# Gate product of the second layer as seven block products (Strassen), with its first two units between the last transposes of the rows, in a two-layer encoder kernel

## What is computed

```python
for i in range(2):
    h = rmsnorm(x, g_pre[i])
    o = mixer_i(h)                      # attention, convolution or Fourier branches, output projection
    x = x + rmsnorm(o, g_post[i])       # called x1 below
    x = x + sigmoid(x @ w_ple_gate[i]) * (p[i] @ w_ple[i])
```

## Time and profile before

| | |
|---|---|
| median of 3 runs | 2020.82 us |
| profiled execution, its own time | 2011.86 us |
| its span, first to last instruction | 2010.1 us |
| PE busy | 1934.5 us, 96% |
| PE weight load, DVE, ACT, POOL busy | 80%, 54%, 32%, 37% |
| mean granted TensorE clock | 0.990 |
| last product of the output projection ends, gate's last embedding ends | 1829.7, 2006.1 us |

### The profile page before, as it was taken

The page is one execution under the profiler, slowest core; times in us unless marked ns, Lnnn a source line. Parts: engine busy times, 40 slices in busy tenths (PEclk is TensorE's granted clock), DMA queues, the critical chain, the costliest instruction groups (busy, mean ns, idle before and its releaser), DMA issues. The chain is left out here.

```text
span 2010.1 us, 26242 instructions
## 1 busy us (share of the span) xinstructions
PE 1934.5 (96%) x9856; PEld 1615.1 (80%) x9856; DVE 1094.2 (54%) x1639; ACT 652.4 (32%) x1339; POOL 745.0 (37%) x540
## 2 busy tenths in 40 slices
PE   4999999999989999999989999999999999999999
PEld 3788888887889788788777888777989897887887
DVE  5599999736768217415753100366777773265211
ACT  6111212211668332212222111123777774322000
POOL 0111121132687444545533132223635362544521
PEclk9999999999989999999999999999999999999999
DMA  4102333443566546534311222484221224565322
GB/s 170 64 11 68 137 93 108 143 143 112 181 236 229 199 160 229 183 107 145 116 52 40 72 85 89 155 308 140 59 54 48 62 78 145 176 240 185 114 94 80
DMA packets 144176, 256.73 MB, mean 128 GB/s; under 512 B 30593, under 2 KB 69249, under 8 KB 144066
## 3 DMA queue, kind: packets, MB, share of 16 engines
q1 hardware_dynamic: 144066, 255.25, 38.6%
HBM read 166.93 MB, written 88.28 MB: 127 GB/s over the span
## 5 line engine op out<-in xcount | busy, mean ns | idle before, releaser
L589 DVE SCALAR_TENSOR_TENSOR ie_acc<-ie_u,ie_wconv,ie_acc 128x1551 f32<-128x1551 f32 x120 | 249.7, 2081 | 3.2
L187 POOL TENSOR_TENSOR w_lo_part<-w_raw,w_hi_part 128x1024 fp32r<-128x1024 f32 x24 | 67.8, 2827 | 331.1 <-ACT w_hi_part L179 331.1
L169 POOL TENSOR_TENSOR w_hi_part<-w_raw,zero 128x1024 fp32r<-128x1024 f32 x56 | 108.0, 1928 | 174.6 <-DMA w_raw<-wall 167.6
L1425 PE MATMUL op_ps<-w_hi_part,rows_hi 128*128 128x512 f32 x384 | 157.1, 409 | 5.1 <-DVE rows_lo L1153 2.6
L1632 DVE SCALAR_TENSOR_TENSOR gt_x<-gt_tanh,gt_ps_p 128x512 f32<-128x512 f32 x48 | 33.0, 688 | 230.1 <-PE gt_ps_p L1665 211.2
L324 PE MATMUL ie_ps<-rows_hi,w_hi_part 128*128 128x512 f32 x384 | 150.4, 392 | 3.9 <-DVE w_lo_part L553 3.8
L1652 PE MATMUL gt_ps<-w_hi_part,rows_hi 128*128 128x512 f32 x384 | 153.3, 399 | 0.0
L1425 PE MATMUL op_ps<-w_hi_part,rows_lo 128*128 128x512 f32 x384 | 152.4, 397 | 0.0
L324 PE MATMUL ie_ps<-rows_hi,w_lo_part 128*128 128x512 f32 x384 | 152.3, 397 | 0.0
L1425 PE MATMUL op_ps<-w_lo_part,rows_hi 128*128 128x512 f32 x384 | 152.0, 396 | 0.0
L1652 PE MATMUL gt_ps<-w_lo_part,rows_hi 128*128 128x512 f32 x384 | 152.0, 396 | 0.0
(11 more groups left out here) (254 smaller groups left out, 4926.8 us busy)
## 6 DMA issues: line engine op xcount, KB each, us to landing
w_raw<-wall SPq DMA_DIRECT2D x84, 512.0 KB, 4.8
op_in<-x SPq DMA_DIRECT2D x24, 512.0 KB, 4.4
x<-op_in SPq DMA_DIRECT2D x24, 512.0 KB, 3.0
gt_x<-x SPq DMA_DIRECT2D x48, 256.0 KB, 3.3
pro_x<-x SPq DMA_DIRECT2D x12, 512.0 KB, 8.8
op_in<-attn SPq DMA_DIRECT2D x24, 256.0 KB, 3.0
o_half<-op_ost SPq DMA_DIRECT2D x24, 256.0 KB, 2.2
gt_p_raw<-p_fm SPq DMA_DIRECT2D x48, 128.0 KB, 3.2
```

What stands on the lines that cost most here:

```text
L169: pool.tensor_tensor(hi, raw, g.zero[:, 0:1].broadcast_to([P, QCOLS]), ALU.add).then_inc(g.w_hi, 1)
L187: pool.tensor_tensor(g.W[1][:, pair % 2, off:off + QCOLS], g.raw[:, n % 2, :], g.W[0][:, pair % 2, off:off + QCOLS].bitcast(F32), ALU.subt ...
L589: dve.scalar_tensor_tensor(acc[:], ubuf[:, cc, s:s + CW], wconv[:, cc, s:s + 1], acc[:], ALU.mult, ALU.add).then_inc(taps, 1)
L1425: mm = pe.matmul(product_at(c * NT + t), g.XT[a][:, k, t * P:(t + 1) * P], w_at(g, name, m, k * HALF, HALF), start=k + a + m == 0, stop=k ...
```

## The change

The second layer's gate product is computed by Strassen's method in Winograd's form. x1 is cut in four blocks (first 768 rows against last 768, first 512 of the inner dimension against last 512), and so is W (rows against columns, B11 to B22). Seven products of 768x512 by 512x512 take the place of eight, in passes named after their left operand: A11, A12, S2, S3, S1, S4, A22. A pass has 6 units (a tile of 128 rows by 512 columns), so there are 42 units of 12 matrix instructions (4 pieces by 3) in place of 24 of 24. The passes A12, S1, S4 and A22 complete a result each time; the embedding (6 instructions), tanh and the two DVE instructions follow there, 24 times as before.

What else it adds or moves:
- In `out_proj` ACT copies the turned x1 whole (`copy_rows`) in place of `split_hi`, DVE's `split_lo` is gone, and both split the left operand of the first seven units there, one per step from step 6 on. Afterwards each engine's loop over n splits the left operand of unit n+7 (`high` on ACT, `low` on DVE) into a ring of 8.
- DVE also makes the sums S1 to S4 of x1's blocks (24 instructions of 128x512, both inputs in SBUF), and adds the units up: 42 instructions of 128x512 with one input in PSUM (`consume`).
- The right operands T2, T3, T1 and T4 are sums of W's blocks. SP loads blocks of 1 MB and 512 KB for them, POOL sums (10 instructions of 128x1024), ACT takes the high part (10, `w_high`), POOL the low part (10). The second half of the gate weights is no longer split as before.
- PE turns the last two tiles of x1 after units 0 and 1 of the gate.
- SP's list has the block loads between the stores of finished units.

The core of the diff:

```diff
+SEVEN = ("A11", "A12", "S2", "S3", "S1", "S4", "A22")
+PAIRS_OF_TILES = NT // 2
+NU = len(SEVEN) * PAIRS_OF_TILES
+RING, AHEAD = 8, 7
...
+    def source(self, n):
+        i, j = divmod(n, PAIRS_OF_TILES)
+        name = SEVEN[i]
+        return {"A11": self.row(0, 0, j), "A12": self.row(0, 1, j), "S2": self.s2(j), "S3": self.row(0, 0, j),
+                "S1": self.row(1, 0, j), "S4": self.row(0, 1, j), "A22": self.row(1, 1, j)}[name]
+    def wait_source(self, eng, n):
+        i, j = divmod(n, PAIRS_OF_TILES)
+        name = SEVEN[i]
+        if name in ("S3", "S1"):
+            eng.wait_ge(self.summed_k, 2 * j + 1 + (name == "S1"))
+        elif name in ("S2", "S4"):
+            eng.wait_ge(self.summed, 2 * j + 1 + (name == "S4"))
+        else:
+            eng.wait_ge(self.copied, j + 1 + (PAIRS_OF_TILES if name == "A22" else 0))
+    def part(self, m, n):
+        r = n % RING
+        return self.g.XT[1][:, 4 * m:4 * m + 4, r * P:(r + 1) * P]
+    def high(self, act, n):
+        self.wait_source(act, n)
+        if n >= RING:
+            act.wait_ge(self.mm, n - RING + 1)
+        act.copy(self.part(0, n), self.source(n)).then_inc(self.hi, 1)
+    def low(self, dve, n):
+        dve.wait_ge(self.hi, n + 1)
+        dve.tensor_tensor(self.part(1, n), self.source(n), self.part(0, n).bitcast(F32), ALU.subtract).then_inc(self.lo, 1)
+    def sum_k(self, dve, j):
+        dve.wait_ge(self.lo, j + 1)
+        dve.wait_ge(self.copied, PAIRS_OF_TILES + j + 1)
+        dve.tensor_tensor(self.row(0, 0, j), self.row(0, 0, j), self.row(1, 0, j), ALU.subtract).then_inc(self.summed_k, 1)
+        dve.tensor_tensor(self.row(1, 0, j), self.row(1, 0, j), self.row(1, 1, j), ALU.add).then_inc(self.summed_k, 1)
+    def sum_s2(self, dve, j):
+        dve.wait_ge(self.summed_k, 2 * j + 1)
+        dve.tensor_tensor(self.s2(j), self.row(1, 1, j), self.row(0, 0, j), ALU.subtract).then_inc(self.summed, 1)
+    def sum_s4(self, dve, j):
+        dve.wait_ge(self.lo, PAIRS_OF_TILES + j + 1)
+        dve.wait_ge(self.summed, 2 * j + 1)
+        dve.tensor_tensor(self.row(0, 1, j), self.row(0, 1, j), self.s2(j), ALU.subtract).then_inc(self.summed, 1)
...
+                if step >= 2 and blocks:
+                    copy_rows(step - 2)
+                    if step >= 6 and step - 6 < 7:
+                        blocks.high(act, step - 6)
...
+                if step >= 6 and blocks and step - 6 < 7:
+                    blocks.low(dve, step - 6)
...
+            def turn_x1(pe, t):
+                pe.wait_ge(x1_rows, 3 * (t + 1))
+                if t < 2:
+                    pe.wait_ge(lo, 2 * NT)
+                elif blocks:
+                    pe.wait_ge(blocks.copied, t - 1)
+                else:
+                    pe.wait_ge(lo, 2 * NT + t - 1)
+                rows_turned(pe, inb[:, t % 2, 2:4].rearrange("p a c -> p (a c)"), full_at(t), g.ident[:], 8).then_inc(turned, 1)
+            g.turn_x1 = turn_x1
+            for step in range(NT if blocks else NT + 2):
...
+        SLOT = {"A11": (1, 0), "A12": (1, 1), "S2": (0, 0), "S3": (0, 1), "S1": (1, 0), "S4": (0, 0), "A22": (1, 1)}
+        BLOCK = {"T2": (0, 0), "T3": (0, 1), "T1": (1, 0), "T4": (1, 1), "B22": (0, 0)}
+        READY = ["T2", "T3", "T1", "T4", "B22"]
+        OF_PASS = {"S2": "T2", "S3": "T3", "S1": "T1", "S4": "B22", "A22": "T4"}
...
+            sp.wait_ge(bl.mm, 1)
+            sp.wait_ge(g.w_ready, QBASE[PIDX[f"gate{l}_a"] + 1])
+            load_block("T3", B22)
+            load_raw(B12, 0)
+            load_block("T2", B11)
+            sp.wait_ge(bl.copied, NT)
+            load(0)
+            load(1)
+            ple.load_weights(sp, 1)
+            for n in range(NU):
+                e = whole(n)
+                if n == 7:
+                    sp.wait_ge(bl.mm, 6)
+                    load_block("T1", B12)
+                    load_raw(B11, 1)
+                if n == 12:
+                    sp.wait_ge(bl.mm, 12)
+                    load_block("T4", B21)
+                    load_raw(B22, 2)
+                if n == 18:
+                    sp.wait_ge(bl.mm, 18)
+                    load_block("B22", B22)
+                if e is None:
+                    continue
+                if e + 2 < E:
+                    load(e + 2)
+                sp.wait_ge(x2_rows, 2 * (e + 1))
+                c, t = COLS[e // PAIRS_OF_TILES], e % NT
+                sp.dma_start(tiles_of(g.y, t)[:, c * HALF:(c + 1) * HALF], x2[:, e % 3]).then_inc(stored[e % 3], 16)
...
+            for q in range(2):
+                pool.wait_ge(block_in["T3"], 16)
+                pool.wait_ge(raw_in[q], 16)
+                pool.tensor_tensor(quarter("T3", q), quarter("T3", q), g.raw[:, q], ALU.subtract).then_inc(w_summed, 1)
+                pool.wait_ge(block_in["T2"], 16)
+                pool.wait_ge(w_summed, 2 * q + 1)
+                pool.tensor_tensor(quarter("T2", q), quarter("T2", q), quarter("T3", q), ALU.add).then_inc(w_summed, 1)
+            low("T2", 0)
+            low("T2", 1)
+            ple.split_rows(pool, 2)
+            ple.split_rows(pool, 3)
+            low("T3", 0)
+            ple.split_rows(pool, 4)
+            low("T3", 1)
+            ple.split_rows(pool, 5)
+            for q in range(2):
+                pool.wait_ge(block_in["T1"], 16)
+                pool.wait_ge(raw_in[q], 32)
+                pool.tensor_tensor(quarter("T1", q), quarter("T1", q), g.raw[:, q], ALU.subtract).then_inc(w_summed, 1)
+            ple.split_rows(pool, 6)
+            ple.split_rows(pool, 7)
+            for q in range(2):
+                pool.wait_ge(block_in["T4"], 16)
+                pool.wait_ge(w_summed, 5 + q)
+                pool.tensor_tensor(quarter("T4", q), quarter("T4", q), quarter("T1", q), ALU.add).then_inc(w_summed, 1)
+            pool.wait_ge(w_summed, 8)
+            for q in range(2):
+                low("T1", q)
+            for q in range(2):
+                pool.wait_ge(raw_in[q], 48)
+                pool.tensor_tensor(quarter("T4", q), quarter("T4", q), g.raw[:, q], ALU.subtract).then_inc(w_summed, 1)
+            ple.split_weights(pool, 1)
+            for name in ("T4", "B22"):
+                for q in range(2):
+                    low(name, q)
+            for e in range(8, E):
+                ple.split_rows(pool, e)
...
+            W_HIGH = {4: ("T2", 0), 5: ("T2", 1), 6: ("T3", 0), 7: ("T3", 1), 14: ("T1", 0), 15: ("T1", 1),
+                      20: ("T4", 0), 21: ("T4", 1), 22: ("B22", 0), 23: ("B22", 1)}
...
+            for n in range(NU):
+                if n == PAIRS_OF_TILES:
+                    for done in g.x1_out:
+                        act.wait_ge(*done)
+                if n + AHEAD < NU:
+                    bl.high(act, n + AHEAD)
+                if n < PAIRS_OF_TILES:
+                    act.wait_ge(bl.mm, n + 1)
+                    act.copy(U[:, n], ps[:, n % 4]).then_inc(u_copied, 1)
+                if n in W_HIGH:
+                    w_high(*W_HIGH[n])
+                if whole(n) is not None:
+                    tanh(whole(n))
...
+            for n in range(NU + 1):
+                if n + AHEAD < NU:
+                    bl.low(dve, n + AHEAD)
+                j = n - 4
+                if n < PAIRS_OF_TILES:
+                    bl.sum_k(dve, n)
+                if 0 <= j < PAIRS_OF_TILES:
+                    bl.sum_s2(dve, j)
+                if PAIRS_OF_TILES <= n < NU:
+                    consume(n)
+                if 0 <= j < PAIRS_OF_TILES:
+                    bl.sum_s4(dve, j)
+                if n and whole(n - 1) is not None:
+                    row(whole(n - 1))
...
+            def product(n):
+                i, j = unit(n)
+                name = SEVEN[i]
+                slot, half = SLOT[name]
+                bank_free(n)
+                pe.wait_ge(bl.lo, n + 1)
...
+            def embedding(e):
+                c = COLS[e // PAIRS_OF_TILES]
+                if e == 0:
+                    pe.wait_ge(bl.copied, NT)
+                pe.wait_ge(ple.p_split, 2 * (e + 1))
+                pe.wait_ge(ple.w_split, 2 * (c + 1))
+                if e >= 2:
+                    pe.wait_ge(x2_rows, 2 * (e - 2) + 1)
...
+            for n in range(NU):
+                product(n)
+                if n < 2:
+                    g.turn_x1(pe, NT - 2 + n)
+                if whole(n) is not None:
+                    embedding(whole(n))
...
-            gate(g, 1, ple)
+            gate_seven(g, ple)
```

185 lines of the change are left out of this document (175 added, 10 removed).

## The result

The changed kernel takes 2026.88 us (median of 20 runs, 2018.97 to 2031.35), the kernel before, run beside it, 2018.78 us (20 runs, 2012.25 to 2029.17). The ratio is 1.0035, 95% interval 1.0022 to 1.0048: slower by 7.1 us (the plain medians differ by 8.1), and more than the 0.2% that can be told from no change. An eighth of the gate product's arithmetic is gone, and the kernel got slower.

What follows compares the result with a forecast made beforehand. PE was taken as the bound, 96% busy. Span 1987.7 us without waits, plus 23.2 for two waits, 1.8 clock and 1.5 third wait gave 2014.2, 4.1 over before; laid on the median 2020.8: 2025 us, range 2010 to 2034.

Steps and rivals of the forecast that it cites:

- first wait: PE at unit 8's embedding waits 15.8 us for DVE's L2001, delayed by six POOL passes; bounds 1.5 to 20.
- The case that was called likeliest: Whole kernel measured slower than before, above 2024.9 us; chance 0.45.
- The work without waits: Gate from 1829.74 us: 153.4 us of PE for units, embeddings and turns, then a tail; span 1987.7 us.
- PE busy down some 23 us in the gate: Sign to look for in the gate: PE's busy time falls some 23 us.
- The turns of the port: DVE and POOL alternate on two-SBUF-input instructions, 2.2 us of DVE per POOL pass; L1214, L1220, L1221, L1225, L1230 lengthened.
- The second wait: Unit 9's embedding waits for the fourth p, landing 9.4 us after issue; both waits together put PE 23.2 us behind.
- The clock: PE's lowered clock after idling costs 1.8 us behind the second wait; behind the first it is hidden.
- The third wait: Unit 26's embedding waits for POOL's ninth p behind its weight passes, 1.5 us, between 0 and 4.
- the cheap port: Rival at the first wait: port costs DVE little, wait 1.5 to 7 us, median 2008 to 2016; chance 0.24.
- The p does not queue: Rival: fourth p not queued behind T1's blocks, or third wait absent; 4 to 5 us less, 2020 to 2021; 0.25.
- DVE falling behind in S1: Rival in the S1 pass: DVE takes 7.9 us against 4.18 per unit, 10 us lost, 2032 to 2036; chance 0.16.

Runs made afterwards that it cites:

- best1: Changed kernel with act_late's edit, T1's transfers on ACT's queue, the ninth p split earlier, S1 sums in DVE's turns 11 to 16; ratio 0.9985.
- best3: Changed kernel with T1's transfers and p's high parts on ACT, T2/T3 high parts and T4 low parts later, S1 sums in DVE's turns 14 to 19; ratio 1.0003.
- act_late: Changed kernel with ACT's high parts of T2 and T3 in turns 8 to 11, POOL's row splits between sums and low parts; ratio 1.0018.
- no_sums: Changed kernel with T2 and T3 summed over 16 of 1024 columns only, same waits and signals, gate result not the reference's; ratio 0.9997.
- gap: Changed kernel with a semaphore wait between DVE's sums L1220 and L1221, some 0.1 us of gap, six times; ratio 1.0033.
- best2: best1 with the S3 sums three turns later, S2 and S4 one turn later and ahead of the low part; ratio 0.9998.
- turns_first: Changed kernel with PE turning the last two tiles of x1 before unit 0, as in the kernel before; ratio 1.0051.
- best5: Changed kernel with T1's transfers and p's high parts on ACT, T2/T3 high and T4 low parts later, four embedding banks, earlier p loads; 2008.05 us, ratio 0.9946.

## Why the prediction was right

2025.0 was predicted, 2026.88 measured; counted against the kernel before, +4.1 us of span predicted, +7.1 measured, +6.3 in the profiled stage. That the two totals lie only 1.9 us apart is in part luck: the 2020.8 from which the prediction counted, 3 runs, is 2.0 above the 2018.78 of 20 runs, and at the first wait errors of both signs cancel. The case that was called likeliest is the one that came. By its steps:

- **The work without waits.** 153.4 us of PE and 4.6 of tail, 158.0. After: a unit 2.80, an embedding 1.38 or 1.46, the last one's end at 2022.47 and the span's 4.3 us later. Right.
- **"PE busy down some 23 us in the gate"** was wrong as a sign to look for, though the 23 us of the sum were right. PE's busy time in the stage fell by 11.1, from 172.1 to 161.0. The 23.0 were counted against elapsed time, which before held 4.2 us of waits at the head; and time at a slow clock counts as busy. Behind the three waits it added 2.5 + 2.7 + 1.8 us: 153.4 + 7.0 is 160.4.
- **The first wait**, 15.8 predicted, 13.0 measured, released by DVE's L2001, as it said. PE was there at 1870.75, predicted 1860.3 + 10.4. L2001 ended at 1883.6 where 1886.5 was predicted. The step erred in three places that partly cancel. DVE's instructions start 0.60 us apart and not 0.68, which over 31 is 2.5 us. POOL's passes cost DVE 14.3 in the sum; measured are four meetings of 2.0 to 2.2 us (L1230, L1220, L1221, L1225) and 1.4 in three smaller ones, 9.9 together. One reason is that the sum took POOL's turns for alternating from the first pass on, where POOL stood 4.4 us until DVE left a gap. The sum had no term for DVE idling behind ACT, which waited for POOL, 3.9 us.
- **The turns of the port**: L1220, L1221, L1225 and L1230 have means of 1.12, 1.11, 1.75 and 2.69 us in that stretch, L1968, with PSUM, 0.69 in the whole stage. L1214 was to be long too and was not (0.68 in three of four; 1.27 in the fourth), since in those turns POOL still stood.
- **The second wait.** The p landed 10.7 us after the first result, predicted 9.4. Both waits together: 21.6 us behind, predicted 23.2.
- **The clock**, 1.8 predicted behind the second wait, 2.7 measured. That the clock falls behind the third wait too was left out: 2.10 + 3.91 in place of 1.38 + 2.80, 1.8 us.
- **The third wait**, 1.5 predicted, 1.8 measured, released by POOL's split of the ninth p as said.

With the measured terms: 158.0 - 0.3 + 21.6 + 2.7 + 1.8 + 1.8 is 185.6 us, against 186.6 measured (the rest is in embeddings that take 1.46 to 1.67 us). The prediction had 184.5.

Of the rivals, the cheap port (waits of 1.5 to 7 us, released by the same instruction) is ruled out in this kernel by the 2.8 us rows and the wait of 13.0. While POOL's first sum stood, 4.4 us, the port did cost DVE nothing. The Trainium skill's rule (SBUF — State Buffer, Who interferes with whom) is that issue order decides who blocks. The turns that the two took afterwards agree with it; that first stand does not, since the pass had started at 1855.13 and seven DVE instructions that started after it, 1855.41 to 1859.02, ran ahead of it. "The p does not queue" is out in so far as the p is delayed behind T1's blocks, 7.8 us against 3.2; whether by the queue is open. DVE falling behind in S1 did not happen in the changed kernel, where the S1 sums are early. It did in best1, which moved those sums: its 3.6 us at unit 26, in the S1 pass, are a wait for DVE's L2012. best3's waits for DVE are in the S3 pass.

## What to carry to other kernels

When a faster product moves work to DVE and POOL, add up not each engine's busy time but the turns both take on two-SBUF-input instructions: here each full meeting with a weight pass of 2.4 us cost DVE 2.0 to 2.2 us, and most of the 23 us gained on PE were lost at the head of the stage, where a list of thirty DVE instructions stood ahead of the first result. Before reordering such a list, look for slack on the consumer's side: two spare PSUM banks, loads issued further ahead and two earlier high parts together brought 7 us of stage, while five reorderings moved the waits to other units as often as they removed them. A big transfer issued just ahead of a small one that someone waits for is to be put where nobody is waiting, and a wait of PE can cost 2 to 3 us more than itself, in slow clock behind it.

## What the runs showed of the hardware that was not expected

- A POOL instruction can stand for several DVE instructions. In the changed kernel its first sum arrives in the ninth of a row of DVE instructions that start 0.60 us apart, all with two SBUF inputs, and stands 4.4 us, until the row's first gap, 0.1 us (6.83 in place of 2.4; 6.92 in act_late, and 4.52 for 16 columns in no_sums). So it goes in all eight kernels in which it arrives there.
- No gap is needed, though, where the DVE row is young. Where the pass arrives in the first instruction of a row, behind a break, it gets in right behind that one, although the next starts only 0.6 us later: in gap, best1, best2, best3 and here in turns_first, whose first sum takes 2.61 us.

```profile
1854.67 2.61 POOL L1896 TENSOR_TENSOR w_sum<-w_sum,w_raw 128x1024 f32<-128x1024 f32 x1 [13.78 <-DMA w_raw<-wall]
```
```profile
1854.32 0.69 DVE L1214 TENSOR_TENSOR rows_lo<-bl_rows,rows_lo 128x512 fp32r<-128x512 f32 x1 [0.90 <-ACT rows_lo L1210]
1854.93 2.90 DVE L1220 TENSOR_TENSOR bl_rows<-bl_rows 128x512 f32<-128x512 f32 x1
```

- Afterwards the two alternate although DVE shows no gap. What decides between standing and getting in at once is open: no run here varies how long DVE's row is by itself.
- Back to back, DVE's 128x512 instructions last 0.68 us each and start 0.60 apart, so that a chain of them is an eighth shorter than the sum of its rows.
- After 13 us of idling PE's first embedding took 2.9 us and the product 3.8 (1.38 and 2.80 usual), after 6.3 us 2.9 and 4.0, after 1.8 us 2.1 and 3.9. The shortest wait cost as much in slow clock as in waiting. Not every short wait does: in best5 the granted clock stayed at 1.00 behind unit 8's 0.83 us, and from 1896 to 1904 behind the 2.52 us ahead of unit 16, which is longer than 1.8. What decides it is open.
